# Placing 384 row dot products inside VectorE's top-16 choices, in both expert layers

## The reference, cut to what matters

```python
def peer_ffn(h, wq, k1, k2, u, v):
    q = (ht @ wq).reshape(n_tok, PEER_HEADS, PEER_QDIM)
    s1 = jnp.einsum('thd,kd->thk', q[..., :PEER_HALF], k1)
    s2 = jnp.einsum('thd,kd->thk', q[..., PEER_HALF:], k2)
    t1, i1 = lax.top_k(s1, PEER_TOPK)                  # 16 of 128, twice
    t2, i2 = lax.top_k(s2, PEER_TOPK)
    cand_s = (t1[..., :, None] + t2[..., None, :])...  # 16 x 16 sums
    top_s, pos = lax.top_k(cand_s, PEER_TOPK)          # 16 of 256
    idx = jnp.take_along_axis(cand_i, pos, axis=-1)
    g = jax.nn.softmax(top_s, axis=-1)
    ...
        ue = jnp.take(u, ib, axis=0)
        ve = jnp.take(v, ib, axis=0)
        act = jax.nn.gelu(jnp.einsum('td,thkd->thk', hb, ue), approximate=False)
        return jnp.einsum('thk,thkd->td', gb * act, ve)
```

## Time and profile before

| | us |
|---|---|
| median of 3 runs (lowest, highest) | 4365.14 (4363.71, 4365.69) |
| the profiled execution, its own time | 4366.11 |
| its span | 4364.3 |
| TensorE matmul busy | 3709.9 (85%) |
| VectorE busy | 3194.6 (73%) |
| ScalarE busy | 1331.1 (30%) |
| GpSimd busy | 1639.4 (38%) |

### The profile page before, as it was taken

One profiled execution on the slowest core, in us unless ns is written; L12 is line 12 of the kernel. 1 busy time (PEld: TensorE's weight loads), 2 busy tenths in 40 slices (PEclk: granted clock), 3 DMA queues, 4 the chain that ended last, 5 costly groups with the idle time before them and its releaser, 6 DMA issues. The chain is left out here.

```text
span 4364.3 us, 59379 instructions
## 1 busy us (share of the span) xinstructions
PE 3709.9 (85%) x19545; PEld 1930.6 (44%) x19545; DVE 3194.6 (73%) x6186; ACT 1331.1 (30%) x1722; POOL 1639.4 (38%) x1191
## 2 busy tenths in 40 slices
PE   6898779789969595979999978977998888699996
PEld 1555565454525252434444423434555455344442
DVE  2547644539878787679999976853679898588887
ACT  0326521221212021222332215841234343233332
POOL 0400000230323233257777821202334435277774
PEclk8999989899989797989999989988999999799998
DMA  5946654585999898899999972122569888799995
GB/s 207 348 152 236 215 165 149 196 302 190 318 346 326 327 346 308 317 350 403 404 404 404 403 268 74 60 89 73 169 227 330 295 309 300 290 338 345 346 344 219
DMA packets 416426, 1188.55 MB, mean 272 GB/s; under 512 B 40112, under 2 KB 126960, under 8 KB 409584
## 3 DMA queue, kind: packets, MB, share of 16 engines
q1 hardware_dynamic: 241244, 639.88, 40.9%
q0 software_dynamic: 110592, 402.70, 25.6%
q10 hardware_dynamic: 64420, 143.77, 8.6%
HBM read 988.98 MB, written 197.23 MB: 272 GB/s over the span
## 5 line engine op out<-in xcount | busy, mean ns | idle before, releaser
L2094 PE MATMUL ex_R<-ex_vl,hh 128*128 128x512 f16 x1792 | 683.0, 381 | 0.0
L1664 PE MATMUL ca_A<-hh,ca_us 128*128 128x512 f16 x2048 | 625.2, 381 | 13.0 <-ACTq L1731 11.4
L2094 PE MATMUL ex_R<-hl,hh 128*128 128x512 f16 x1792 | 542.6, 382 | 81.6 <-DVE hh L2108 60.2
L1632 POOL DMA_INDIRECT ca_ug<-in_peer_u_rows,chosen_rows x288 | 286.1, 994 | 710.2 <-DVE ca_ug L1788 592.8
L2125 DVE SCALAR_TENSOR_TENSOR ex_sum<-ex_vg,ex_share,ex_sum 128x1024 f32<-128x1024 f32 x384 | 493.1, 1284 | 9.8 <-DVE ex_share L2117 6.0
L2022 POOL DMA_INDIRECT ex_vg<-in_peer_v_rows,ex_index x384 | 374.4, 975 | 204.5 <-DVE ex_ar L2103 97.9
L1788 DVE SCALAR_TENSOR_TENSOR ca_ug<-ca_ug,ca_hp 128x1024 f32<-128x1024 f32 x288 | 346.1, 1216 | 107.7 <-DMA ca_ug<-in_peer_u_rows,chosen_rows 106.0
L1664 PE MATMUL ca_A<-hh,ca_uh 128*128 128x384 f16 x1024 | 343.7, 336 | 78.1 <-DVE ca_ul L1758 55.2
L1705 ACT ACTIVATE ca_ga<-ca_A 128x512 f32<-128x512 f32 (+1 forms) x256 | 139.4, 544 | 832.9 <-PE ca_A L1664 753.9
L1664 PE MATMUL ca_A<-hl,ca_us 128*128 128x512 f16 x1024 | 390.7, 382 | 0.0
L2133 DVE TENSOR_TENSOR ACC<-ACC,ex_R 128x512 f32<-128x512 f32 x448 | 305.7, 682 | 112.4 <-PE ex_R L2094 109.2
(11 more groups left out here) (384 smaller groups left out, 7123.3 us busy)
## 6 DMA issues: line engine op xcount, KB each, us to landing
ex_vr<-in_peer_v SPq DMA_DIRECT2D x256, 512.0 KB, 9.5
ca_us<-u_parts SPq DMA_DIRECT2D x128, 512.0 KB, 6.3
ca_ur<-in_peer_u SPq DMA_DIRECT2D x128, 512.0 KB, 5.5
gates<-ca_stage ACTq DMA_DIRECT2D x28, 2048.0 KB, 11.8
acts<-ca_ga ACTq DMA_DIRECT2D x128, 256.0 KB
ex_gr<-gates SPq DMA_DIRECT2D x32, 1024.0 KB
ex_ar<-acts SPq DMA_DIRECT2D x128, 256.0 KB, 11.5
acts<-ca_ga ACTq DMA_DIRECT2D x128, 192.0 KB, 4.0
```

The costliest lines, as they stand in the source:

```text
L1632: nc.gpsimd.indirect_dma_start(ug[x % UG][:, :], None, u_rows, bass.IndirectOffsetOnAxis(ap=chosen_rows[:, x:x + 1], axis=0)).then_inc(ug_ ...
L1664: last = nc.tensor.matmul(A[b][:, a:a + w], lhs[:, k, :], rhs[:, k, a:a + w], start=(k == 0 and x == 0), stop=(k == KD - 1 and x == 2))
L2094: last = nc.tensor.matmul(R[(NP * q + y) % BANKS][:, :], lhs[q][:, x, o:o + P], rhs[q][:, x, h * 512:h * 512 + 512], start=(x == 0 and n = ...
```

## The change

The dots are taken out of their rows and put singly between the operations of a choice (`between` counts work in units and issues the next `low` and the next dot when their share is reached). Some go beside the first dense choice, where there were none.

| | layer 0 before, after | layer 1 before, after |
|---|---|---|
| chunks in `pre` | 12, 16 | 16, 16 |
| chunks in `tail` | 4, 0 | 4, 4 |
| dots beside the first dense choice | 0, 14 | 0, 24 |
| dots in a gates phase | 40, 44 | 32, 24 |
| dots at a later choice | 32, 22 | 16, 16 |
| `midway_at` | 7, 8 | 10, 10 |

The sums stay 4 x 40 + 3 x 32 = 14 + 4 x 44 + 3 x 22 = 256 and 3 x 32 + 2 x 16 = 24 + 3 x 24 + 2 x 16 = 128. The load of `iota` goes from SyncE's queue to ScalarE's, behind the scores, and VectorE casts it within the first choice. In the `pre` chunks `begin` stands one chunk ahead of `midway` in layer 0.

```diff
-PRE = (12, 16)
+PRE = (16, 16)
-    ahead, beside, midway_at = {4: (12, 16, 7), 3: (17, 19, 10)}[nt]
+    ahead, beside, midway_at = {4: (12, 16, 8), 3: (17, 19, 10)}[nt]
-    by_step, BY_HEAD = {1: ([2] * STEPS, 2), 2: ([2, 3] * (STEPS // 2), 4)}[NG]
+    FIRST_DOTS, by_step, BY_CHOICE = {1: (24, [1, 2] * (STEPS // 2), 16), 2: (14, [3, 3, 2, 3] * (STEPS // 4), 22)}[NG]
 ...
     def chunk_of_dot(x):
-        n, r = divmod(x, BY_TILE)
+        if x < FIRST_DOTS:
+            return pre + ahead * x // FIRST_DOTS
+        n, r = divmod(x - FIRST_DOTS, BY_TILE)
         if r < BY_STEPS:
             step = max(e for e in range(STEPS) if upto_step[e] <= r)
             return pre + ahead + n * CT + beside * (step + 1) // STEPS
-        return pre + (n + 1) * CT + ahead // 2 + ahead * (r - BY_STEPS) // (2 * BY_HEAD * PH)
+        return pre + (n + 1) * CT + ahead * (r - BY_STEPS) // BY_CHOICE
 ...
-                        if x == ((g + 1) * (pre // NG) - 1 if NG > 1 else 3 * pre // 4 - 1):
+                        if x == ((5, 13)[g] if NG > 1 else 3 * pre // 4):
+                            begin(g)
+                        if x == ((6, 14)[g] if NG > 1 else 3 * pre // 4 - 1):
                             midway(g)
-                        if x == (pre // 2, pre - 1)[g] + (pre // 4 if NG == 1 else 0):
-                            begin(g)
 ...
                         for x in range(n):
                             step.mark(nc.vector.max_index(places[x][0], values[x][0], src[x]))
                             step.mark(nc.vector.match_replace(src[x], values[x][0], src[x], -3.0e38))
+                            between(each[1])
                         settle()
-                        if between is not None:
-                            between(2)
 ...
-                    def choices(n, tile, first_chunk, chunks, gathered=None, first_dot=None):
+                    def choices(n, tile, first_chunk, chunks, gathered=None, first_dot=0, dots_here=0):
+                        rows, heads = range(2 * PH), range(PH)
+                        by_row, by_head = (2, 7, 2, 4), (2, 4, 2, 2)
+                        whole = sum(by_row) * len(rows) + 30 + sum(by_head) * len(heads) + 110
+                        at = {"work": 0, "lows": 0, "dots": 0}
+
+                        def between(work):
+                            at["work"] += work
+                            while at["lows"] < min(chunks, chunks * at["work"] // whole + 2):
+                                low(tile, first_chunk + at["lows"])
+                                at["lows"] += 1
+                            while at["dots"] < dots_here * at["work"] // whole:
+                                dot_product(first_dot + at["dots"])
+                                at["dots"] += 1
 ...
                         dve.sem_inc(chosen, 1)
-                        if first_dot is not None:
-                            for h in range(PH):
-                                for x in range(BY_HEAD):
-                                    dot_product(first_dot + BY_HEAD * h + x)
-                                beside_choice(6 + h)
+                        between(20)
 ...
-                    choices(NG, 0, pre, ahead)
                     dve.wait_ge(rows_ready, 1)
+                    choices(NG, 0, pre, ahead, None, 0, FIRST_DOTS)
                     for n in range(nt - 1):
                         gates_of(n)
-                        choices(n + 1 + NG, n + 1, pre, ahead, None, n * BY_TILE + BY_STEPS)
+                        choices(n + 1 + NG, n + 1, pre, ahead, None, FIRST_DOTS + n * BY_TILE + BY_STEPS, BY_CHOICE)
```

More of the change, by code:

```diff
@@ L1635, in _ @@
                     issued = 0
-                    for x in range(PCH):
+                    for x in range(0 if ready else PCH):
                         if x >= RING:
@@ L1758, in low, with best16 @@
                             nc.vector.tensor_tensor(ul[j][:, :, :], ur[j][:, :, :], uh[j][:, :, :], ALU.subtract).then_inc(u_cut[j], 1)
-                    def best16(src, values, places, between=None):
+                    def best16(src, values, places, each, between):
                         n = len(src)
@@ L1765, in best16 @@
                             step.mark(nc.vector.max(values[x][0], src[x]))
+                            between(each[0])
                         settle()
-                        if between is not None:
-                            between(1)
                         for x in range(n):
@@ L1771, in best16 @@
                             step.mark(nc.vector.match_replace(src[x], values[x][0], src[x], -3.0e38))
+                            between(each[1])
                         settle()
-                        if between is not None:
-                            between(2)
                         for x in range(n):
                             step.mark(nc.vector.max(values[x][1], src[x]))
+                            between(each[2])
                         settle()
@@ L1779, in best16 @@
                             step.mark(nc.vector.max_index(places[x][1], values[x][1], src[x]))
+                            between(each[3])
                         settle()
@@ L1805, in pick_numbers @@
                         step.wait()
+                        between(25)
                         for x in (1, 2):
@@ L1825, in pick_numbers @@
                             step(nc.vector.tensor_tensor(sel[:, 0:2, q * PH * 8:(q + 1) * PH * 8], ends[:, :, :, 0], ends[:, :, :, 1], ALU.add))
-                    def choices(n, tile, first_chunk, chunks, gathered=None, first_dot=None):
-                        work_before = [0, 34, 100, 165, 235, 315]
-                        if first_dot is not None:
[L1830 to L1835, removed]
-                        beside_choice(0)
+                            between((25, 40)[q])
+                    def choices(n, tile, first_chunk, chunks, gathered=None, first_dot=0, dots_here=0):
[11 more added lines that the diff above has]
+                                at["dots"] += 1
+                        between(0)
                         step.start(n, CHOICE_STEPS)
@@ L1877, in choices @@
                         assert step.n == CHOICE_STEPS, step.n
-                        if first_dot is not None:
-                            for h in range(PH):
-                                for x in range(BY_HEAD):
-                                    dot_product(first_dot + BY_HEAD * h + x)
-                                beside_choice(6 + h)
+                        between(20)
+                        assert at == {"work": whole, "lows": chunks, "dots": dots_here}, (at, whole)
                     dve.sem_inc(hot_done, 2)
                     dve.sem_inc(prod, 2)
-                    dve.wait_ge(iota_in, 16)
-                    gstep(nc.vector.tensor_copy(iota[:, :], iota32[:, :]))
-                    gstep(nc.vector.tensor_copy(iota2[:, :, :], iota32[:, :].unsqueeze(2).broadcast_to([P, P, 2])))
                     def turn(n, k):
```

33 lines of the change are left out of this document (17 added, 16 removed).

## The result

| | before | changed |
|---|---|---|
| median (lowest, highest), us | 4365.15 (4363.71, 4365.69) | 4328.49 (4323.64, 4331.53) |
| the profiled execution, us | 4366.11 | 4331.53 |
| TensorE / VectorE busy, us | 3709.9 / 3194.6 | 3731.4 / 3186.7 |
| granted clock | 0.927 | 0.934 |

The changed kernel takes 0.9916 of the time before, 95% interval 0.9905 to 0.9928: 36.7 us less, where 77 less were forecast. The sign and the range held; the size is half.

What follows compares the result with a forecast made beforehand. Layer 0 was taken as bound by TensorE's gates work and its wait behind VectorE's dots, layer 1's gates phases by VectorE. From 4366.1 us, layer 0's -37 and layer 1's -40 gave 4289, median 4288 us; range 4212 to 4352.

Steps and rivals of the forecast that it cites:

- The bound: Layer 0's later choices: TensorE idle some 45.6 us behind `turn`, which stands behind VectorE's row of dots waiting for gathers.
- Layer 0's choice, idle 20 in place of 45.6: Layer 0's three later choices: TensorE's idle gap shrinks by 25.6 us each, -76.8 us in all.
- Gates phases +6 each: Layer 0's four gates phases: 44 dots for 40 cost +6 us a phase, +24 us in all.
- the first part +20.7: Layer 0's start: four more chunks in `pre` move everything behind by +20.7 us and hide the 14 new dots.
- the end -5: Layer 0's end without tail: next block 24 us behind the last gate matmul instead of 29, -5 us.
- the 110 that I had named as a sign of being wrong: Layer 0: gates phases above 110 us would show the forecast wrong; 102 to 106 us would show it right.
- `midway` costs nothing in layer 0: Layer 0's choice with `midway_at` 8: a few us perhaps lost while TensorE would wait for `chosen` anyway, term 0.
- Layer 1's gates phases, -27.4: Layer 1's three gates phases: VectorE is full, so 24 dots for 32 save 9.1 us each, -27.4 us.
- Layer 1's later choices, 72 us each: Layer 1's two later choices, 16 dots inside: 72 us in place of 82.5, -10.5 each, -21 us.
- Layer 1's first dense choice, +8: Layer 1's first dense choice: 24 dots, 27.4 us of work on 20.2 us idle, +8 us; bounds +7 and +20.
- Layer 1 gains nothing: Rival: gathers ahead of GpSimd's lows make TensorE wait for `ca_ul` in every layer 1 choice; 4328 us, chance 0.12.
- The stores don't hold up gathers: Rival: layer 0 gaps idle only 5.4 us, gates phases unchanged, layer 1 -45 us; 4215 us, chance 0.17.

Runs made afterwards that it cites:

- eight parts: Changed kernel with each tile's gates stores in eight 1 MB parts spread over the chunks, both layers: 4281.41 us, ratio 0.9829.
- Four buffers: Changed kernel with four output buffers for gelu (`ca_ga`) in layer 1 in place of two: 4312.8 us, ratio 0.9884.
- late dots: Changed kernel with the 16 dots of a later choice in layer 1 only in the choice's second half: 4320.18 us, ratio 0.9896.

## Why the prediction was right in layer 0 and wrong in layer 1

*The bound.* Right: the gap behind `turn` was there to win, and three choices gave 68 us.

*Layer 0's choice, idle 20 in place of 45.6.* Right in mechanism, 3 us a phase too good. VectorE's waits for gathers beside the stores are 20.2 us, where I had 13. I had priced the wait by one landing of 15.1 us; the median in the phase was 9.7, from 4.2 to 19.1. I took 389 GB/s as what the engines carry beside the stores; eight parts reached 401 to 403.

*Gates phases +6 each, the first part +20.7, the end -5.* Right: +5.8, +19.4, -6.2. The second gates phase took 111.8 us, above the 110 that I had named as a sign of being wrong; in seven other runs with the same layer 0 and the stores in four parts it took 103.8 to 111.1. VectorE's waits for gathers in all of layer 0 are 105.3 us (about 117 said).

*`midway` costs nothing in layer 0.* Borne out as time: ScalarE's 11.7 us and TensorE's 10.4 are real waits, but VectorE sets the phase. The waits of TensorE that I had put ahead of the transposes (about 60 us) show up as 23.9 there and 39.3 in front of `ca_A`. That the two add up to my number is luck: I had no wait at `ca_A`.

*Layer 1's gates phases, -27.4.* Right, -26.4.

*Layer 1's later choices, 72 us each.* This is the step that failed. I added up VectorE's work (69.6) and TensorE's (66.1), weighed the stores only as a delay of gathers ("4.4 us, just above the 4.3 beside stores"), and gave ScalarE no term. The phases took 91.1 and 87.6. Without the stores' bytes they take 74.7 and 76.4, so the sum of work was nearly right; the stores cost 16.4 and 11.2 us. Four buffers gave back 10.1 and 6.9 of these, which shows that path, through ScalarE's two buffers and its casts, for that much. The rest was not isolated: with four buffers ScalarE waits for loads of u in place of stores (40.3 us, before 5.2). Layer 0 has the larger wait for `acts` (107.6 us), but no casts hang on ScalarE there, its u chunks come ready, and in the phase read above VectorE's work and its gathers fill the time. That the wait for `acts` costs nothing there is argued from this; no run gave layer 0 more buffers.

*Layer 1's first dense choice, +8.* Measured +15, one of the signs of being wrong that I had named. I set 27.4 us of dots against 20.2 us of idle time as if all of it could be filled. VectorE was busy for 78.30 of 86.3 us, so 8.0 stayed idle, and one wait is 6.7 of it: the first gather is issued at 3137.55, 3.5 us behind `chosen`, since GpSimd has a low ahead of it, and the first dot waits for its landing. My upper bound was also mis-added: 27.4 + 16 - 20.2 is +23, not +20.

*The rivals.* "Layer 1 gains nothing" has the time that came out, 4328, but not its mechanism: TensorE's waits for `ca_ul` from GpSimd are not what holds the choices, and putting the lows first made it 24 us slower. "The stores don't hold up gathers" was wrong for four parts (waits of 20.2 us), and eight parts, at 4281, go a little over half of the way from 4365 to its 4215. The Trainium skill's formula (DMA: Bandwidth & Descriptors, "Anatomy of one DMA — SWDGE (gpsimd) path") gives an estimate of 3.2 us for a gather; it was not seen in any phase of either layer, where the minima are 4.2 us and up.

**Left open.** Eight parts are smaller and come more evenly over the chunks; no run separates the two. The stores were never moved to another queue at unchanged times of issue. Why late dots leave 83.3 and four buffers 81 us, and not 75, is explained only in part: ScalarE still waits 61.1 and 42.3 us for `acts`, and with four buffers 40.3 for loads of u.

## What to carry to other kernels

Before moving work beside a stretch of large stores, list every transfer that shares the engines or the queue with them, down to the smallest, and ask which engine stands still when that one is late and what else is in that engine's program; an engine that is 30% busy can be the one. When the moved work brings its own traffic, the stores' grain has to be chosen anew: the same split cost 29 us in the kernel before the change and gave 47 in the changed one. A sum of busy times bounds a phase from below only.

## What the runs showed of the hardware

- Behind a 2 MB store in the same hardware queue, a 192 KB store took up to 12.9 us to land (changed kernel, layer 1's first later choice; the trace has the landing of every second one). With the gates stores moved to the other queue it took 8.8 at most in that phase, while the 512 KB loads of that queue went from a median of 8.4 to 12.8 us.
- Four 2 MB stores in a phase left the DMA engines at 326 to 362 GB/s, shares of 0.87 and 0.92; eight stores of 1 MB for the same bytes reached 370 at 0.97 in layer 1 and 401 at 1.01 in layer 0, and with four buffers in layer 1 384 at 0.98. So the share that was missing was no limit of the engines; that the requests came late because their issuers stood waiting is my reading, not a measurement.
